# The next full expert tile's transposes go ahead of the weighing, on VectorE

## What is computed

```
u, v: [16384, 1024]; expert, gates: [tokens, 128] from a router
act = gelu(einsum('td,ted->te', h, u[expert]))
out = einsum('te,ted->td', gates * act, v[expert])
```

## Time and profile before

| | us |
|---|---|
| median of 3 runs | 3789.88 (3787.57 to 3791.18) |
| the profiled execution | 3787.01, of which its span 3785.1 |
| TensorE matmuls busy | 3619.8 (96%) |
| TensorE weight loads busy | 3232.5 (85%) |
| VectorE busy | 2531.1 (67%) |
| ScalarE busy | 1549.9 (41%) |
| mean granted clock of TensorE | 0.976 of 2.4 GHz |

### The profile page before, as it was taken

The page is one execution under the profiler, slowest core; times in us unless marked ns, Lnnn a source line. Parts: engine busy times, 40 slices in busy tenths (PEclk is TensorE's granted clock), DMA queues, the critical chain, the costliest instruction groups (busy, mean ns, idle before and its releaser), DMA issues.

```text
span 3785.1 us, 64666 instructions
## 1 busy us (share of the span) xinstructions
PE 3619.8 (96%) x22310; PEld 3232.5 (85%) x22310; DVE 2531.1 (67%) x5382; ACT 1549.9 (41%) x3138; POOL 304.4 (8%) x430
## 2 busy tenths in 40 slices
PE   8999999999999999999999999999899999999998
PEld 7878889988788899887888888888779888888887
DVE  6535327666353376655798888888536998888887
ACT  4132127441321274313344554555334345544554
POOL 0201100002011000000045000000000180000000
PEclk9999999999899999999999999999999999999999
DMA  7632248776222487612433666666444416666664
GB/s 212 169 87 65 59 123 255 235 207 162 79 65 65 128 253 226 156 56 85 138 93 115 190 192 189 190 191 185 113 116 127 133 57 199 190 192 189 189 192 132
DMA packets 652324, 567.68 MB, mean 150 GB/s; under 512 B 66251, under 2 KB 597722, under 8 KB 651738
## 3 DMA queue, kind: packets, MB, share of 16 engines
q1 hardware_dynamic: 646884, 544.95, 50.8%
q0 software_dynamic: 4960, 19.93, 1.6%
q10 hardware_dynamic: 278, 0.08, 0.0%
HBM read 553.30 MB, written 9.44 MB: 149 GB/s over the span
## 4 chain that ended last, share of the span: by engine, by line
PE 71%; DVE 17%; ACT 5%; issue 4%; DMA 2%; SPq 0%; DVEq 0%; ACTq 0%
PE bank L795 17%; PE bank L815 13%; PE bank L1282 10%; PE bank L1295 4%; PE bank L1296 3%; PE bank L1297 3%; PE bank L1258 3%; PE bank L791 2%; ACT v_high L1944 2%; DVE tab L3009 2%; DVE v_low L3015 2%; DVE bank L2987 2%; PE bank L1243 1%; PE bank L1037 1%; PE bank L1047 1%
## 5 line engine op out<-in xcount | busy, mean ns | idle before, releaser
L795 PE MATMUL bank<-hT,ring 128*128 128x256 f32 (+2 forms) x2064 | 470.8, 385 | 8.1 <-DVE hT L2328 5.6
L795 PEld LDWEIGHTS bank<-hT,ring 128*128 128x128 f32 (+2 forms) x2064 | 388.9, 190 | 73.9 <-issue 15.7
L1282 PE MATMUL bank<-t_high,u_parts 128*128 128x256 f32 x3072 | 427.4, 282 | 4.2 <-DVE u_parts L2994 4.2
L1295 PE MATMUL bank<-v_high,w_low 128*128 128x512 f32 x1024 | 411.1, 401 | 19.4 <-DVE v_low L3015 13.8
L1282 PEld LDWEIGHTS bank<-t_high,u_parts 128*128 128x128 f32 x3072 | 404.8, 189 | 22.5 <-issue 5.0
L1296 PE MATMUL bank<-v_low,w_high 128*128 128x512 f32 x1024 | 407.4, 398 | 0.0
L1297 PE MATMUL bank<-v_high,w_high 128*128 128x512 f32 x1024 | 406.0, 396 | 0.0
L3015 DVE TENSOR_TENSOR v_low<-ring,v_high 128x512 fp32r<-128x512 f32 x512 | 337.2, 690 | 67.8 <-ACT v_high L1944 43.7
L1944 ACT ACTIVATE v_high<-ring 128x512 fp32r<-128x512 f32 x512 | 299.5, 620 | 45.8 <-PE bank L1297 44.2
L1563 ACT ACTIVATE arena<-bank 128x256 f32<-128x256 f32 (+1 forms) x278 | 106.4, 386 | 472.5 <-PE bank L795 265.3
L2131 POOL TENSOR_SCALAR uT<-cst,selT 128x128 f32<-128x128 f32 x256 | 187.5, 742 | 1380.6 <-ACT selT L1885 1375.4
(11 more groups left out here) (430 smaller groups left out, 6326.6 us busy)
## 6 DMA issues: line engine op xcount, KB each, us to landing
ring<-in_peer_v SPq DMA_DIRECT2D x256, 512.0 KB, 3.8
ring<-in_peer_u SPq DMA_DIRECT2D x768, 128.0 KB, 3.7
ring<-in_w_in SPq DMA_DIRECT2D x132, 512.0 KB, 4.0
ring<-in_mlp_up SPq DMA_DIRECT2D x64, 512.0 KB, 4.4
uT<-in_mod_w SPq DMA_DIRECT2D x64, 512.0 KB, 5.0
ring<-in_mlp_down SPq DMA_DIRECT2D x64, 512.0 KB, 4.2
ring<-in_peer_u SPq DMA_DIRECT2D x64, 512.0 KB, 3.7
arena<-in_mod_w POOLq DMA_DIRECT2D x32, 512.0 KB, 4.8
```

Of the source, the lines that this page charges most:

```text
L795: ins = eng.matmul(ps[0:n, 0:width], wv[:, i, :], moving(u * 8 + i), start=(u == 0 and i == 0), stop=(u == count - 1 and i == k - 1))
L1282: ins = eng.matmul(PB[6 + b][:, 0:S], u_parts[:, part, k * P:k * P + P], moving[:, k, :], start=(n == 0), stop=(n == len(products) - 1))
L1295: eng.matmul(ps, w_low[:, b, t], v_high[:, d], start=first, stop=False)
```

## The change

The step j of VectorE's `eight` does the transposes in front of the weighing. Because they now overwrite the PSUM banks directly behind the rests that read them, `turn` waits for the semaphore that those rests count up.

```
 def turn(i, f):
     eng.wait_ge(sem(f"u_full{f % 2}"), ...)
+    if positive(i * 6 + (f + FULL * l)):
+        eng.wait_ge(sem("uL_ready"), i * 12 + (2 * f + 2 * FULL * l))
     for q in range(2):
         eng.transpose(PB[4 + q]..., blocks_of(f, q)).then_inc(sem("u_turned"), 1)
...
 for j in range(8):
     f = FULL_AT.get(j + 1)
     if f is not None and not (isinstance(i, int) and i == 0 and f == 0):
         u_low(i, f)
-    weigh(i, j)
     if f is not None and not (isinstance(i, int) and i == 15 and f == 5):
         turn(i, f + 1)
+    weigh(i, j)
```

## The result

The changed kernel takes 3912.9 us (median of 4, 3908.78 to 3916.68) where the kernel before took 3788.73 beside it: a ratio of 1.0325, 95% interval 1.0311 to 1.0338, 124 us slower. 3916 was forecast. The profiled execution took 3916.68 us, its span 3914.8.

What follows compares the result with a forecast made beforehand. TensorE's work was taken to bound the expert stage; the period grows 2.03 us to 22.10, over 63 periods +128 us, less 1 or 2 per layer, on 3787.0 plus 2.9 for the median: 3916 us, range 3833 to 3945.

Steps and rivals of the forecast that it cites:

- TensorE bounds the stage, its waits are all there is to win: Expert stage: TensorE busy 39.74 of 40 us; reordering can give back at most 46.5 us of waits for v_low.
- No slack for the moved work: VectorE: each moved weighing starts 1.35 us later, against slacks of 1.01 (weighing 0), 1.13 (weighing 2), none (weighing 3).
- The landing at B + 6.27: Next group's tile 1 u rows land then, after rests end at B+5.04; VectorE stands still 1.2 us.
- B: Time origin of the forecast schedule: the end of combine 0, 2415.39 in the kernel before.
- The schedule of one period: Four-tile group in the expert stage: stalls ahead of combines 2, 3 and 0 make the period 22.10 us for 20.07.
- X: Start of combine 2 in the forecast schedule, B + 9.90, where TensorE wants it at B + 8.46.
- The sum: Whole kernel: 2.03 us more in 63 periods, +128 us, less at most 1 or 2 in each layer's first group.
- The wait on its own engine, 0.12: VectorE: waiting for the rests' own ends ahead of transposes makes up 0.12 of each moved weighing's 1.35 us.
- The turn alone: Rival, chance 0.17: no landing wait for u rows, only the later weighings cost, +51 us, 3841.
- Faster: Rival, chance 0.04: weighing 3 starts with its gelu, combine 3's 0.41 us a period goes, 26 us, 3764.
- no change: Rival, chance 0.03: new stalls only take the place of combine 3's 0.41 us, about 3790.
- the clock: Rival, chance 0.06: TensorE's idle gaps drop its clock to 1.2 GHz for a twentieth of the stage, 3980.

Runs made afterwards that it cites:

- The best kernel here: Kernel before with w_low x v_high matmuls first in each combine half and scores starting on half the u rests: 3757.21 us, ratio 0.9916.
- the first two moves alone: Kernel before with only tile 2's transposes ahead of the weighing: 3820.04 us; with only tile 3's: 3811.39 us.
- the kernel with the earlier load: Changed kernel, with SyncE issuing each group's tile 1 u rows ahead of tile 0's v load: 3836.27 us, ratio 1.0121 to before.

## Why the prediction was right

- *TensorE bounds the stage, its waits are all there is to win.* Held. The best kernel here takes a period down to 19.64, and no further. The ceiling of 46.5 us was read too high, for it counts matmuls and weight loads: by the periods (20.07 for 19.63) there were 28 us to win, and 27.9 came in the stages.
- *No slack for the moved work.* Held, and confirmed one by one. Slacks of 1.01 and 1.13 against a weighing 1.35 later gave 29 and 18 us for the first two moves alone, worked out before those runs; 30 and 21 came.
- *The landing at B + 6.27.* Held: in the changed kernel B is 2431.31, the transposes start at 2437.67, B + 6.36. The wait was put at 1.2 and is 1.22 in the steady part; the group shown, with 1.32, is one of the longer ones.
- *The schedule of one period.* 22.10 forecast, 22.05 read. Its stalls: 1.44 ahead of combine 2 (1.46), 0.22 ahead of combine 3 (0.23), 0.49 ahead of combine 0 (0.40), none ahead of combine 1 (none). The one that is off is combine 0's: I let score 1 end 3.15 behind the rests of tile 1 (X + 8.83 against X + 5.68), and it took 3.20 (2428.03 against 2424.83), and from the weighing's start to the combine's first matmul the rows give 2428.43 - 2426.09 = 2.34 for 2.37.
- *The sum.* Here some luck is in it. The period of 22.10 is 0.11 over the middle one of the first layer (21.99), some 7 us in all. And 63 groups was a miscount: in each of two layers 31 of the 32 groups have a next one, which makes 62 and the sum 2 us less. Against that, the first groups of each layer wait longer (one wait of 4.1) where I had taken 1 or 2 us off. In the stages 122.7 us came for the 126 of 62 periods.
- *The wait on its own engine, 0.12.* The transposes start 0.03 behind the rests (2424.86 against 2424.83), as the row of L2316 said. No run took the wait alone away, since the transposes may not overwrite banks that the rests still read, so its price of 0.12 is shown by the rows and not by a time.
- *The turn alone*, a rival here, is the kernel with the earlier load: 3841 worked out, 3836 measured.
- *Faster, no change, the clock.* The chain of combine 3 is indeed bound by buffers that combine 2 frees: its stall, 0.30 + 0.11 before, is 0.23 + 0.11 after (0.22 + 0.11 worked out). The granted clock stayed 1.00 in the steady stretch, with 36.78 of 40 us busy and gaps of 1.3 us. What the Trainium skill, TensorE: Matmul & The Clock Gate, A second HAM failure mode: psum-queue depth-cycling, tells of another kernel, that short idles between groups of matmuls made the clock swing, does not show in that stretch.

## What to carry to other kernels

An engine at 83% may still have no room at one place of its order: write down, for each step that others wait for, when it could serve and when it is wanted, and compare the difference with what is to be put ahead of it. A wait that ends a long idle time on an engine off the critical path (86.0 us on ScalarE) is no reason to move the work that ends it. When work is moved forward, look where its data land, and when a stall is cured, ask what is late next: two of the cures here gave half or nothing until that was answered. The order in which the waiting engine takes its own work (products that need less first, half waits) gave 33 us; moving the feeding work forward gave only loss. And where a view adds up waits, look whether it counts one stall on two instruction streams, as with the 46.5 and 244.6 us here.

## What the runs showed that was not expected

- A cure can be worth 77 us (the earlier u load with the transposes first) and nothing at all (3788.73 for 3790.39) beside the other order: its worth is that of the wait it stands behind.
- Costs of parts did not add: 30 + 21 + 88 = 139 us singly, 124 together (137.0 and 122.7 in the stages).
- Starting TensorE's score 0.2 us earlier shortened the period from 19.86 to 19.64 with the transposes behind, and not at all (20.02, 20.01) with them ahead.
